# Stick-breaking attention on one Trainium2 core: three fp32r matmuls for each block of weights times v, or one fp32 matmul

## The reference, cut to what matters

```
logits        = q_blk @ k.T * 128**-0.5
log_beta      = log_sigmoid(logits)
log_one_minus = where(causal, log_beta - logits, 0)
suffix        = cumsum(log_one_minus, reverse) - log_one_minus
weights       = where(causal, exp(log_beta + suffix), 0)
y             = weights @ v
```

## Time and profile before

| | |
|---|---|
| three runs | 2737.40, 2738.89, 2738.95 us; median 2738.89 us |
| the profiled execution | 2739.31 us, of which the trace's span is 2737.6 us |
| PE matmul, busy | 2586.8 us, 94% of the span, 13812 matmuls |
| DVE / ACT / POOL, busy | 1597.0 / 1260.3 / 928.9 us (58 / 46 / 34%) |
| granted TensorE clock, mean | 0.97 of full speed |

### The profile page before, as it was taken

One profiled execution on the slowest core, in us unless ns is written; L12 is line 12 of the kernel. 1 busy time (PEld: TensorE's weight loads), 2 busy tenths in 40 slices (PEclk: granted clock), 3 DMA queues, 4 the chain that ended last, 5 costly groups with the idle time before them and its releaser, 6 DMA issues. The chain is left out here.

```text
span 2737.6 us, 38907 instructions
## 1 busy us (share of the span) xinstructions
PE 2586.8 (94%) x13812; PEld 2224.3 (81%) x13812; DVE 1597.0 (58%) x2057; ACT 1260.3 (46%) x2212; POOL 928.9 (34%) x776
## 2 busy tenths in 40 slices
PE   6999999999989999999995999799999999799998
PEld 5788888888768888888885999688777778689997
DVE  7555554545655455555543444689888899534342
ACT  5564333443445433343432221588888878411111
POOL 2434232332444333232321221366666665000000
PEclk8999999999999999999996999999999999899999
DMA  3333333333222323333336444111221122443331
GB/s 101 107 96 127 105 114 117 98 118 101 95 69 88 105 99 119 101 117 114 101 104 192 134 136 154 70 61 68 77 77 46 73 77 77 139 153 111 121 122 62
DMA packets 239712, 283.57 MB, mean 104 GB/s; under 512 B 12048, under 2 KB 189200, under 8 KB 236560
## 3 DMA queue, kind: packets, MB, share of 16 engines
q1 hardware_dynamic: 229008, 265.86, 30.1%
q10 hardware_dynamic: 10624, 16.78, 1.7%
HBM read 190.32 MB, written 92.27 MB: 103 GB/s over the span
## 5 line engine op out<-in xcount | busy, mean ns | idle before, releaser
L720 PE MATMUL in_bank<-in_a_hi,in_w_hi 128*128 128x512 f32 x1988 | 778.3, 392 | 26.5 <-ACT in_o L425 16.8
L722 PE MATMUL in_bank<-in_a_lo,in_w_hi 128*128 128x512 f32 x1988 | 775.5, 390 | 0.0
L723 PE MATMUL in_bank<-in_a_hi,in_w_lo 128*128 128x512 f32 x1988 | 775.4, 390 | 0.0
L720 PEld LDWEIGHTS in_bank<-in_a_hi,in_w_hi 128*128 128x128 f32 x1988 | 374.6, 188 | 107.0 <-ACT in_o L425 17.7
L723 PEld LDWEIGHTS in_bank<-in_a_hi,in_w_lo 128*128 128x128 f32 x1988 | 374.4, 188 | 78.2
L722 PEld LDWEIGHTS in_bank<-in_a_lo,in_w_hi 128*128 128x128 f32 x1988 | 374.8, 189 | 77.3
L407 ACT ACTIVATE in_w_hi<-in_sums 128x512 fp32r<-128x512 f32 x284 | 179.0, 631 | 474.4 <-PE in_bank L723 325.4
L563 DVE TENSOR_TENSOR in_w_lo<-carried_buffer,in_w_hi 128x512 fp32r<-128x512 f32 x213 | 242.0, 1136 | 260.8 <-ACT in_w_hi L407 257.8
L1571 DVE TENSOR_TENSOR_SCAN att_rest<-att_z_ps,att_rest 128x512 f32<-128x512 f32 (+3 forms) x320 | 355.5, 1117 | 47.6 <-ACT att_z_ps L1520 44.8
L1478 POOL TENSOR_TENSOR att_slot<-att_slot,att_rest 128x512 f32<-128x512 f32 (+3 forms) x320 | 305.0, 958 | 216.0 <-DVE att_rest L1571 215.5
L303 POOL TENSOR_TENSOR in_sums<-carried_buffer 128x512 f32<-128x512 f32 x71 | 91.7, 1292 | 698.8 <-DMA carried_buffer<-in_w_in 696.8
(11 more groups left out here) (169 smaller groups left out, 4776.9 us busy)
## 6 DMA issues: line engine op xcount, KB each, us to landing
carried_buffer<-in_w_in SPq DMA_DIRECT2D x144, 512.0 KB, 4.8
uz_T<-in_o SPq DMA_DIRECT2D x32, 256.0 KB, 4.6
va_T<-in_o SPq DMA_DIRECT2D x32, 256.0 KB, 3.5
q_T<-in_o SPq DMA_DIRECT2D x32, 256.0 KB, 3.6
k_T<-in_o SPq DMA_DIRECT2D x32, 256.0 KB, 3.5
vb_T<-in_o SPq DMA_DIRECT2D x32, 256.0 KB, 3.6
zb_T<-in_o SPq DMA_DIRECT2D x32, 256.0 KB, 3.5
ga_T<-in_o SPq DMA_DIRECT2D x32, 256.0 KB, 3.6
```

Of the source, the lines that this page charges most:

```text
L720: pe.matmul(bank[:, :], hi, a_hi[:, i, k], start=opens and k == 0, stop=False, skip_group_check=True)
L722: pe.matmul(bank[:, :], hi, a_lo[:, i, k], start=False, stop=False, skip_group_check=True)
L723: mm = pe.matmul(bank[:, :], lo, a_hi[:, i, k], start=False, stop=k == HALF_K - 1, skip_group_check=True)
```

## The change

In `attention` the turned weights and the turned v are kept as plain fp32, one copy each, written by ACT. DVE's low halves (`copy_lo`) are gone, with their semaphore. PE waits for ACT's copy (`kept`), and each block of weights times v is one matmul with fp32 operands. Logits, scans, splits of q and k, and the order of the list stay as they are, and so do all widths and buffer counts.

```diff
-        v_hi, v_lo = (sc.sb(n, [P, S], F32R) for n in ("v_hi", "v_lo"))
+        v_sb = sc.sb("v_sb", [P, S])
...
-        wT_hi = [sc.sb(f"wT_hi{n}", [P, CW], F32R) for n in range(W_BUFS)]
-        wT_lo = [sc.sb(f"wT_lo{n}", [P, CW], F32R) for n in range(W_BUFS)]
+        wT = [sc.sb(f"wT{n}", [P, CW]) for n in range(W_BUFS)]
...
-                eng.wait_ge(lo_copied, STEPS * h + (t + 1))
+                eng.wait_ge(kept, STEPS * h + (t + 1))
...
-                    act.activation(v_hi[:, e[1] * CW:(e[1] + 1) * CW], t_bank(t)[:, :],
-                                   ACT.Copy).then_inc(hi_copied, 1)
+                    act.activation(v_sb[:, e[1] * CW:(e[1] + 1) * CW], t_bank(t)[:, :],
+                                   ACT.Copy).then_inc(kept, 1)
...
-                    act.activation(wT_hi[k % W_BUFS][:, c0:], t_bank(t)[:, c0:], ACT.Copy).then_inc(hi_copied, 1)
+                    act.activation(wT[k % W_BUFS][:, c0:], t_bank(t)[:, c0:], ACT.Copy).then_inc(kept, 1)
...
-            def copy_lo(h, e, t):
-                dve.wait_ge(hi_copied, STEPS * h + (t + 1))
-                if e[0] == "V":
-                    cols = slice(e[1] * CW, (e[1] + 1) * CW)
-                    dve.tensor_tensor(v_lo[:, cols], t_bank(t)[:, :], v_hi[:, cols].bitcast(F32), ALU.subtract)\
-                        .then_inc(lo_copied, 1)
-                else:
-                    n, c0 = product_of(e) % W_BUFS, max(0, e[2] - QT * e[1]) * P
-                    dve.tensor_tensor(wT_lo[n][:, c0:], t_bank(t)[:, c0:], wT_hi[n][:, c0:].bitcast(F32),
-                                      ALU.subtract).then_inc(lo_copied, 1)
...
-                    elif e[0] in "VB":
-                        copy_lo(h, e, n)
...
-                        ks, hi, lo = slice(kt * P, (kt + 1) * P), wT_hi[n % W_BUFS], wT_lo[n % W_BUFS]
-                        pe.matmul(bank[:, c0:], v_hi[:, ks], hi[:, c0:], start=(kt == 0), stop=False)
-                        pe.matmul(bank[:, c0:], v_hi[:, ks], lo[:, c0:], start=False, stop=False)
-                        pe.matmul(bank[:, c0:], v_lo[:, ks], hi[:, c0:], start=False,
+                        pe.matmul(bank[:, c0:], v_sb[:, kt * P:(kt + 1) * P], wT[n % W_BUFS][:, c0:], start=(kt == 0),
                                   stop=(('B', sup, kt) == b_steps(sup)[-1])).then_inc(product, 1)
```

More of the change, by code:

```diff
@@ L1351, in attention @@
         turned = sc.sem("turned")
-        hi_copied, lo_copied = sc.sem("hi_copied"), sc.sem("lo_copied")
+        kept = sc.sem("kept")
         product = sc.sem("product")
@@ L1530, in body, with keep @@
                     elif e[0] in "VB":
-                        copy_hi(h, e, n)
-            def copy_hi(h, e, t):
+                        keep(h, e, n)
+            def keep(h, e, t):
                 act.wait_ge(turned, STEPS * h + (t + 1))
```

## The result

The changed kernel takes 2744.14 us (median of 14 runs, 2741.11 to 2748.60), the kernel before 2740.61 us over its 14 runs beside it. The ratio is 1.0016, with a 95% interval of 1.0009 to 1.0023: slower by 0.1 to 0.2%, 3.5 us. Forecast were 2766 us with a range from 2742 to 2808. The sign holds and the time lies 2 us inside the range, but the size doesn't hold: +27.5 us against +3.5. By the forecast's own bound of 0.2% (5.5 us) it is the same time. The profiled execution took 2743.56 us with a span of 2741.9, both 4.3 us above those of before.

A forecast was written before the change was run, and what follows sets the result against it. PE was taken to pace the attention. Against the profiled 2739.3 us: +48.6 for the matmul, -9.1 for v's waits, -7 for the hole, -5 for the clock, 2766.8, stated as 2766 us; range 2742 to 2808.

The forecast's parts named there:

- What bounds the kernel: Attention: PE paces a head, busy 70.0 of 75 us with two holes; DVE, at 67.9 us, rarely holds it up.
- The cost of the fp32 matmul: PE, weights times v: 320 plain fp32 matmuls replace 960 fp32r ones, 881 against 680 ns at 512 columns, +48.6 us.
- Four streams with hidden loads: PE: one fp32 matmul streams its columns four times, 855 ns at 512 columns, while its weight loads cost no extra time.
- the second fixed part: PE: 12.9 ns fixed per half of the stationary operand; two make 881 ns at 512 columns, one would make 868.
- The rivals of two streams and of exposed loads: PE: columns streamed twice, about 2650 us (0.12, with single stream); or fp32 weight loads not hidden, 2837 or 2801 us (0.14).
- The waits for v: PE's waits for DVE's low half of v, about one microsecond a head, vanish: -9.1 us.
- The hole: PE's long wait for POOL's low half of k shrinks from 4.0 to about 3 us in seven heads: -7 us.
- The clock: PE's half-speed stretch after each long wait shortens or vanishes: 0 to 18 us possible in seven heads, a quarter taken, -5 us.
- the forecast's case: Whole kernel: four streams with hidden loads, less the gains from v's waits, hole and clock; 2748 to 2780 us, chance 0.65.
- rival 1: PE: an fp32 matmul streams its columns twice, 454 ns at 512 columns, about 2650 us; 0.12, shared with a single stream.
- Rival 3: PE: the extra matmul work falls into time lost anyway, at most 16 us; near 2740 with the clock's full 18 us; 0.07.

## Why the prediction was wrong

- **What bounds the kernel: right.** PE paces the attention. DVE's 172 us less were worth nothing but where PE waited for them.
- **The cost of the fp32 matmul: right in kind, too high by 10 us.** Four streams with hidden loads, two records each. The failed step is the term +201 ns a block, which became +160. Of these 41 ns the larger part lies with what goes: "Three matmuls thus cost 680 ns at 512" was taken from dense rows of another stage, and in the attention they cost 704. The other 17 ns are the second fixed part: 881 were forecast, the rows show 864, about 9 ns above the four streams' 855. The weight loads of the new matmul take 192 ns on average (640 of them), not the 144 ns of the turns, and hide all the same. The rivals of two streams and of exposed loads are both out.
- **The waits for v: right** (-9.1 us; none is left).
- **The hole: right** (21.2 us for seven, 3.03 against the forecast 3.0 us).
- **The clock: mechanism seen, size wrong.** "I take a quarter, -5 us, since 3 of the 4 us of idling stay" is the step that failed. Seven stretches with 2.6 us of lost work each, 18.2 us, became one with 3.3 us and one with 1.7 (half of 6.50 and 3.40 us busy), -13.2 us. The runs show why a quarter was the wrong guess: the stretches don't shrink in proportion to the hole but shorten to half and then vanish, between holes of 3.8 and 1.6 us.
- **Waits for DVE's low halves that no view shows**, which I counted at nothing in the forecast's case: about 4.5 us.
- **DVE's busy time: too low.** 42 us in a head were forecast, 47.1 measured. The low halves' durations add up to 209 us, but neighbouring DVE instructions overlap, and DVE's busy time fell by 172 us only. It cost the forecast nothing, since DVE does not set the pace.
- **A slip in rival 1:** its -0.15 us at 128 columns doesn't follow from its own formula (133 - 370 ns is -0.24 us). That is 3 us in a rival that did not come.

The sum with the measured terms: 38.3 - 9.1 - 6.6 - 13.2 = +9.4 us, and less 4.5 is +4.9; the profiled executions differ by 4.3. So the small difference is the near cancelling of five effects of 4.5 to 38 us, and that the time still lies in the range, by 2 us, is luck: three terms were off, by 10, 8 and 4.5 us, all in one direction. Rival 3 had this end, near 2740 us, at a chance of 0.07. It was right about the clock, but its own mechanism is not what happened: with DVE's low halves kept, the matmul's whole +38 us showed. The forecast priced the clock's full return, but did not join it with a cheaper matmul.

## What to carry to other kernels

One plain fp32 matmul costs about as much as four streams of its columns (864 ns at 512), against 704 ns for the three products of the hi/lo split in fp32r. On PE it pays only where it is narrow (128 columns: 229 ns against 340). At greater widths it could pay only where an engine that it relieves sets the pace, which no run here shows. Before costing an edit of the engine that sets the pace, look for its few long holes and at the granted clock behind them: here the move of one POOL step, which shortens one hole in a head, brought 22 us in the kernel before (2716.89 against 2739.08), as much as the whole change costs at equal clock.

## What the runs showed of the hardware that was not expected

- A hole in PE's work need not be very long to cost the clock, and a little less hole can save all of it: 7 x 3.4 us at half speed with 3.2 us of hole, none with 1.6 us. Between them, holes of one length, 2.2 us, cost the clock in four of seven heads.
- Where the half-speed stretches have their full 6.8 us, a longer hole can be free: 3.8 and 4.4 us gave 549.7 and 549.9 us for seven heads.
- A plain fp32 matmul appears as two weight loads and two matmuls, and takes some 9 to 15 ns more in all than four streams of 0.4176 ns a column (864 against 855 ns at 512, 229 against 214 at 128), while each fp32r matmul in the dense rows takes 13 ns more than one.
